# Routed experts on one core: the down products of a step move between the third and fourth quarter of the next step's up products

## The chip, the core and the metric

The kernel runs on one core of a Trainium2 chip, in one launch. The metric is the device time of that core in microseconds (us): the median of several runs, and beside it one profiled execution from which the rows below are read. PE is TensorE, DVE is VectorE, ACT is ScalarE, POOL is GpSimd and SP is SyncE, which only issues DMAs here.

## What is computed

One decoder layer on 1056 tokens (1024 of a prompt, 32 of samples), in fp32. The change touches only the routed experts of the channel-mixing sub-layer:

```python
D_MODEL, N_EXPERTS, TOP_K, EXPERT_FF = 1024, 64, 8, 256

def swiglu(x, w_gate, w_up, w_down):
    return (jax.nn.silu(x @ w_gate) * (x @ w_up)) @ w_down

# in moe(u, ...): eight experts are chosen for each token, gw holds their gates
def expert_block(args):
    xblk, e = args
    return swiglu(xblk, exp_w_gate[e], exp_w_up[e], exp_w_down[e])
yb = lax.map(expert_block, (xb, block_e)).reshape(NB * MOE_BLOCK, D) * buf_w[:, None]
routed = jnp.zeros_like(u_pad).at[buf_t].add(yb)[:T]
```

## The kernel before

The routed tokens are packed into 78 steps of 128 rows (four quarters of 32 rows, "quads"). In a step the first 32 rows belong to one expert, the next 32 to one that may be another, and the last 64 to one that may be a third. Each step n goes through these pieces; the names are those of the functions in `experts`:

- **gather** (POOL): copies the row numbers of the step (L2611) and issues four indirect DMAs (L2616), which fetch the 128 rows into one of NX = 2 buffers. It waits until DVE has transposed the step that used the buffer.
- **turn_x** (DVE, L2835): waits for the gather and transposes the rows into `xT`.
- **up** (PE, L2694 to L2697): gate and up products in one PSUM bank. KT = 8 slices of the 1024 inputs are taken in order, two slices to a "unit", so there are four units (quarters 0 to 3). Four small matmuls of a slice run side by side, one for each quad. The first quad reads the weights where they were loaded (`k.ring`). The other quads read copies: `second_up` (DVE L2873 for units 1 to 3, ACT L2787 for unit 0) and `third_up` (ACT L2788, units 0 to 3). PE waits at the start of each unit for the copies of that unit.
- **silu** (ACT, L2758) and **hidden** (DVE, L2841): silu of the gate half, times the token's gate and the up half.
- **turn_hid** (PE, L2723): transposes the hidden rows; **copy_hid** (ACT, L2799) moves them to SBUF.
- **copies_down** (DVE, L2889, four copies): the down weights of the second and third expert.
- **down** (PE, L2711 to L2714): the down products. PE waits for copy_hid, copies_down and the copy_y of the step before.
- **copy_y** (ACT L2766 one half, DVE L2852 the other): moves the result to `y_out`, which has two buffers; it waits until the add of the step before last has landed.
- **add** (POOL, L2636): an indirect DMA that adds the 128 rows to `y_rows` in HBM. It waits for the landing of the add before it, since two adds may meet in a row.

Every engine's order is written by hand; nothing is scheduled by a tool. On PE the order of one step is turn_hid(n-1), up(n), down(n-1). On DVE it is hidden(n), the three copies for up(n+1), copy_y(n-1), copies_down(n), turn_x(n+2). On ACT it is silu(n), copies for up(n+1) units 0 and 1, copy_y(n-1), copy_hid(n), copies for units 2 and 3. On POOL a gather(n) is followed by add(n-3). Each engine works through its list in order, and a wait holds all that stands behind it.

Which expert a quad uses is known only at run time. So DVE and ACT read slot numbers into registers (`value_load`, L2660, shown as TENSOR_LOAD on the engines' queues DVEq and ACTq). On DVE a step reads five of them, all just ahead of hidden. Steps 2 to 75 run on DVE in a loop of two steps a pass (37 passes), on ACT and PE in similar loops.

Weights come through SP (`reload`): a ring of NW = 4 slots holds gate and up weights, a ring of ND = 5 the down weights. SP waits until the last step of expert e-4 has finished its up products (`up_done`), issues gate and up of expert e (L2115), then reports the expert before, e-1, as ready (`up_ready`, L2554, then `down_ready`) once its loads have landed, waits for `down_done` of expert e-5 and issues the down weights of e. copies_up on ACT and DVE wait for `up_ready` of the newest expert of their step. So an expert becomes ready at the earliest when the last step of the expert three before it has ended its up products.

Of the kernel before, what the change touches and what calls it, by code (L numbers as in the profile page):

```python
# [21 lines left out]
KT = D // P  # L22
# [81 lines left out]
def wait_before_addressed(eng, sem, value, passed):  # L104


    eng.wait_ge(sem, value)
    eng.sem_inc(passed, 1)
# [1840 lines left out]
SLOT = 3 * KT * FF  # L1949
NW = 4  # L1950
# [555 lines left out]
NX = 2  # L2506
# [3 lines left out]
def experts(k):  # L2510
# [35 lines left out]
    with nc.Block() as block:  # L2546
# [57 lines left out]
        def _(g):  # L2604
# [32 lines left out]
                                     in_=y_out[:, u, :], in_offset=None, bounds_check=3 * T - 1, oob_is_err=False, compute_op=ALU.add).then_inc(added, 16)  # L2637

            def run(first, last):
                for n in range(first, first + NX + 1):  # L2640
                    gather(n, n % NX)
                for n in range(first, first + NX - 1):
                    gather(n + NX + 1, (n + 1) % NX)
                    add(n, n % 2)
                loops = (last - first) // NX
                with g.Fori(1, loops - 1) as j:
                    for r in range(NX):
                        gather(j * NX + (first + NX + r), (first + r) % NX)
                        add(j * NX + (first - 1 + r), (1 + r) % 2)
                for n in range(first + loops * NX, last):  # L2650
                    gather(n, n % NX)
                    add(n - NX - 1, (n - 1) % 2)
                for n in range(last - NX - 1, last):
                    add(n, n % 2)
                g.wait_ge(added, 16 * last)
            over_ranges(g, run)
# [18 lines left out]
        def _(pe):  # L2675
# [6 lines left out]
            def up(n, u, off):  # L2682
                pe.wait_ge(x_turned, n + 1)
                gate_up = k.ring[:, bass.ds(off, DOWN)].rearrange("p (g k f) -> p k g f", g=2, f=FF)
                out = ps[:, 2 + u, :].rearrange("p (g f) -> p g f", f=FF)
                for j in range(KT):
                    unit, part = divmod(j, 2)
                    cols = slice(part * FF, (part + 1) * FF)
                    if part == 0:
                        pe.wait_ge(up_by_act, 5 * n + (unit + 2))  # L2690
                        if unit:
                            pe.wait_ge(up_by_dve, 3 * n + unit)
                    edges = dict(start=(j == 0), stop=(j == KT - 1))
                    pe.matmul(out[0:QUAD], xT[:, u, j, 0:QUAD], gate_up[:, j], **edges)  # L2694
                    pe.matmul(out[QUAD:HALF], xT[:, u, j, QUAD:HALF], third_up[unit][:, :, cols], **edges)  # L2695
                    for lo in (HALF, HALF + QUAD):
                        ins = pe.matmul(out[lo:lo + QUAD], xT[:, u, j, lo:lo + QUAD], second_up[unit][:, :, cols], **edges)  # L2697
                    if part and j < KT - 1:
                        ins.then_inc(up_part, 1)
                ins.then_inc(up_done, 1)  # L2700

            def down(n, u, off):
                pe.wait_ge(hid_copied, n + 1)
# [27 lines left out]
            def step(n, u):  # L2731
                off = first_of(n)
                off_before = first_down_of(n - 1)
                turn_hid(n - 1, 1 - u)
                up(n, u, off)
                down(n - 1, 1 - u, off_before)

            def run(first, last):
                up(first, 0, first_of(first))
# [15 lines left out]
        def _(act):  # L2755
# [21 lines left out]
            def registers(n):  # L2777
                return newest_of(act, n), up_offsets_of(act, n)
# [25 lines left out]

            def run(first, last):
                copies_up(first, registers(first), range(4))

                def step(n, u, y=True):
                    regs = registers(n + 1)
                    silu(n, u)  # L2810
                    copies_up(n + 1, regs, (0, 1))
                    if y:
                        copy_y(n - 1, 1 - u)
                    copy_hid(n, u)
                    copies_up(n + 1, regs, (2, 3))
                step(first, 0, False)
                step(first + 1, 1)
                step(first + 2, 0)
                with act.Fori(1, (last - first) // 2 - 1) as j:
                    for r in range(2):  # L2820
                        step(j * 2 + (first + 1 + r), (1 + r) % 2)
                silu(last - 1, 1)
                copy_y(last - 2, 0)
                copy_hid(last - 1, 1)
                copy_y(last - 1, 1)
            over_ranges(act, run)
# [3 lines left out]
        def _(v):  # L2830
# [44 lines left out]
            def copies_up(n, newest, off):  # L2875
                wait_before_addressed(v, up_ready, newest + 1, dve_passed)
                for unit in (1, 2, 3):
                    second_up_unit(n, off, unit)

            def copies_down(n, newest, offs):  # L2880
                wait_before_addressed(v, down_ready, newest + 1, dve_passed)
# [10 lines left out]
            def run(first, last):  # L2892
                turn_x(first, 0, first % NX, first // NX)
                if first == 0:
                    for t in range(SH_DOWN + TAIL_ON_ACT, NT):
                        drain_tail(t)
                copies_up(first, newest_of(v, first), up_offsets_of(v, first)[0])
                turn_x(first + 1, 1, (first + 1) % NX, (first + 1) // NX)

                def step(n, u, x, times, y=True, turn=True):  # L2900
                    newest, offs = newest_of(v, n), down_offsets_of(v, n)
                    newest_up, off_up = newest_of(v, n + 1), column_of(v, n + 1, 0, (NW - 1) * SLOT)
                    hidden(n, u)
                    copies_up(n + 1, newest_up, off_up)
                    if y:
                        copy_y(n - 1, 1 - u)
                    copies_down(n, newest, offs)
                    if turn:
                        turn_x(n + 2, u, x, times)
# [4 lines left out]
                fixed(first, y=False)  # L2914
# [7 lines left out]
                fixed(last - 2, turn=False)  # L2922
                newest, offs = newest_of(v, last - 1), down_offsets_of(v, last - 1)
                hidden(last - 1, 1)
                copy_y(last - 2, 0)
# [187 lines left out]
```

## Time and profile before

| | us |
|---|---|
| median of 3 runs | 2782.24 (2778.79 to 2784.44) |
| the profiled execution's own time | 2782.99 |
| its span, first to last instruction | 2781.2 |
| routed experts: first up product to first up product of the last step | 1811.7 to 2684.5 |
| PE busy over the span | 2620.3 (94%) |

The granted TensorE clock over the span was 0.97 of full speed. The profile is read by stage: what the change is worth lies between 1811 and 2705 us, where PE is the engine with the most work, so the view of what PE waits for there is read first, and then the order of time of one step on each engine.

### The profile page before, as it was taken

To read this page: it belongs to the slowest core of one execution; us is meant where nothing else is said; L and a number is where in the kernel's file an instruction comes from. 1 tells how busy PE (TensorE), PEld (TensorE's weight loads), DVE (VectorE), ACT (ScalarE), POOL (GpSimd) and SP (SyncE) were. 2 spreads that over 40 slices of the span, in tenths; PEclk is the share of its full clock that TensorE was granted. 3 is DMA by queue.
4 is the path that set the end of the run, shared out by engine and by line. 5 is a ranking of instruction groups with operands and counts; after the bars stand their busy time and mean duration, and the time that the engine had idled before them with its cause. 6 is when DMAs were issued, how large, how long until landed. Compare 5 with 4: busy or idle time off the path is not lost. (4 is left out here: it accounts for less than half of the span.)

```text
span 2781.2 us, 48997 instructions
## 1 busy us (share of the span) xinstructions
PE 2620.3 (94%) x16668; PEld 1450.8 (52%) x16669; DVE 1369.1 (49%) x2153; ACT 929.7 (33%) x1404; POOL 730.1 (26%) x860
## 2 busy tenths in 40 slices
PE   7997999998999899999999979899999999999988
PEld 4564888874666656666666646533333333233334
DVE  3333332333757587872211147356666655556644
ACT  3213333333424210001100022155555555555541
POOL 1000211210534100000000001355555555555530
PEclk8998999999989999999999989999999999999998
DMA  6530100011011111211210423299888998999946
GB/s 249 214 121 15 27 16 16 16 54 49 24 31 46 32 35 29 70 35 35 97 34 16 172 90 117 96 315 312 291 280 286 348 338 279 341 309 355 319 109 247
DMA packets 161847, 407.77 MB, mean 147 GB/s; under 512 B 19139, under 2 KB 106255, under 8 KB 133433
## 3 DMA queue, kind: packets, MB, share of 16 engines
q1 hardware_dynamic: 135521, 336.95, 33.0%
q0 software_dynamic: 26208, 69.27, 10.4%
q8 instruction: 71, 1.16, 0.2%
q14 instruction: 47, 0.39, 0.0%
HBM read 343.19 MB, written 75.95 MB: 151 GB/s over the span
## 5 line engine op out<-in xcount | busy, mean ns | idle before, releaser
L2694 PE MATMUL ps<-big 128*32 x1248 | 551.9, 595 | 2.4 <-DVE big L2873 1.6
L2695 PE MATMUL ps<-xT,big 128*32 128x512 f32 x1248 | 551.9, 595 | 0.0
L2616 POOL DMA_INDIRECT big<-u_rows,big x312 | 324.4, 1040 | 139.4 <-issue 71.3
L1760 PE MATMUL ps<-big 128*128 128x352 f32 x1152 | 346.7, 461 | 5.7 <-SPq L1696 5.7
L2788 ACT ACTIVATE xT<-big 128x1024 f32 x312 | 311.0, 1047 | 0.0
L2694 PEld LDWEIGHTS ps<-big 128*32 128x32 f32 x1248 | 136.7, 110 | 332.3 <-issue 332.1
L1760 PEld LDWEIGHTS ps<-big 128*128 128x128 f32 x1152 | 219.7, 191 | 129.1 <-SPq L1696 6.1
L2711 PE MATMUL ps<-big 128*32 x624 | 282.2, 595 | 3.2 <-DVE xT L2889 3.2
L2712 PE MATMUL ps<-xT,big 128*32 128x512 f32 x624 | 282.2, 595 | 0.0
L849 PE MATMUL ps<-big 128*128 128x352 f32 x576 | 205.6, 463 | 2.1 <-DMA big<-in_w_in 2.0
L1304 PE MATMUL ps<-big 128*128 128x352 f32 x576 | 185.2, 469 | 10.2 <-DVE big L1524 7.6
L2636 POOL DMA_INDIRECT y_rows<-big x78 | 140.4, 1800 | 141.3 <-DVE big L2852 99.4
L1774 PE MATMUL ps<-big 128*128 128x352 f32 x576 | 174.4, 459 | 1.6 <-DVE big L1894 1.6
L512 PE MATMUL ps<-big 128*128 128x352 f32 x576 | 173.2, 461 | 0.0
L2711 PEld LDWEIGHTS ps<-big 128*32 128x32 f32 x624 | 68.8, 110 | 190.3 <-issue 190.3
L2841 DVE SCALAR_TENSOR_TENSOR big<-big,ps 128x256 f32<-128x256 f32 x78 | 53.3, 684 | 230.3 <-issue 168.9
L2714 PE MATMUL ps<-pick,big 128*32 128x512 f32 x624 | 161.3, 595 | 0.0
L2714 PE MATMUL ps<-big 128*32 128x512 f32 x624 | 161.3, 595 | 0.0
L2835 DVE STREAM_TRANSPOSE big<-big 128x1024 f32<-128x1024 f32 x78 | 96.8, 1242 | 121.2 <-DMA big<-u_rows,big 121.1
L1864 DVE SCALAR_TENSOR_TENSOR big<-big 128x1024 f32<-128x1024 f32 x120 | 154.0, 1284 | 4.7
L2000 POOL MEMSET big<- 128x1 f32 x1 | 0.1, 98 | 578.3 <-POOLq L1699 578.3
L2758 ACT ACTIVATE big<-ps 128x256 f32<-128x256 f32 x78 | 29.9, 383 | 357.2 <-PE ps L2697 357.2
(621 smaller groups left out, 5038.5 us busy)
## 6 DMA issues: line engine op xcount, KB each, us to landing
big<-in_exp_w_gate SPq DMA_DIRECT2D x64, 1024.0 KB, 6.8
big<-in_exp_w_up SPq DMA_DIRECT2D x64, 1024.0 KB, 9.4
big<-in_exp_w_down SPq DMA_DIRECT2D x64, 1024.0 KB, 10.4
big<-in_ada_w SPq DMA_DIRECT2D x24, 1024.0 KB, 7.8
big<-in_w_in SPq DMA_DIRECT2D x48, 512.0 KB, 4.0
x_keep<-xT SPq DMA_DIRECT2D x2, 4224.0 KB, 16.1
y_rows<-pick SPq DMA_DIRECT2D x16, 512.0 KB, 14.3
big<-y_rows SPq DMA_DIRECT2D x16, 512.0 KB, 12.6
```

The lines of the kernel that those rows point to most:

```text
L512: ins = pe.matmul(ps[:, 3 * u + c, 0:CW], ring[:, s, j, u * P:(u + 1) * P], k.hT[:, j, c * CW:(c + 1) * CW], start=(j == 0), stop=(j == KT ...
L849: ins = pe.matmul(ps[:, F0 + u % 2, 0:CW], ring[:, f % 3, j, :], k.hT[:, j, c * CW:(c + 1) * CW], start=(j == 0), stop=(j == KT - 1))
L1304: ins = pe.matmul(ps[:, bank, 0:CW], ring[:, tile_of[kind, y] % 3, x, :], k.hT[:, x, cs], start=(x == 0), stop=(x == KT - 1))
L1760: ins = pe.matmul(ps[:, c, 0:CW], ring_g[:, q % 2, j, :], k.hT[:, j, c * CW:(c + 1) * CW], start=(j == 0), stop=(j == KT - 1))
L1774: ins = pe.matmul(ps[:, 3 + c, 0:CW], ring_v[:, q % 2, j, :], branch[n][:, j, c * CW:(c + 1) * CW], start=(j == 0), stop=(j == 3))
L2616: g.indirect_dma_start(out=x_rows[:, u, x * 256:(x + 1) * 256], out_offset=None, in_=u_quarters, in_offset=bass.IndirectOffsetOnAxis(idx_i ...
L2694: pe.matmul(out[0:QUAD], xT[:, u, j, 0:QUAD], gate_up[:, j], **edges)
L2695: pe.matmul(out[QUAD:HALF], xT[:, u, j, QUAD:HALF], third_up[unit][:, :, cols], **edges)
L2711: pe.matmul(out[0:QUAD], hidT[:, u, j, 0:QUAD], k.down_ring[:, bass.ds(off + (j * D + half * 512), 512)], **edges)
L2712: pe.matmul(out[QUAD:HALF], hidT[:, u, j, QUAD:HALF], third_down[j][:, cols], **edges)
L2714: ins = pe.matmul(out[lo:lo + QUAD], hidT[:, u, j, lo:lo + QUAD], second_down[j][:, cols], **edges)
L2788: act.activation(third_up[unit], up_columns(third, unit), ACT.Copy).then_inc(up_by_act, 1)
```

## The change

It changes the order of the lists in `experts` and nothing that is computed.

- PE: `up` takes the units that it is to do. A step is now up(n) units 0 and 1, turn_hid(n-1), up(n) unit 2, down(n-1), up(n) unit 3.
- ACT: silu(n), the copy for unit 3 of up(n+1), copy_hid(n), the copies for units 0 to 2 of up(n+2), copy_y(n). It reads registers twice in a step, three values ahead of silu as before and three for step n+2 ahead of copy_hid.
- DVE: hidden(n), the copy for unit 3 of up(n+1), copies_down(n), turn_x(n+2), the copies for units 1 and 2 of up(n+2), copy_y(n). Four registers are read ahead of hidden, two ahead of turn_x.
- POOL: a gather(n) is followed by add(n-4) instead of add(n-3).

```diff
             def run(first, last):
-                for n in range(first, first + NX + 1):
+                for n in range(first, first + NX + 2):
                     gather(n, n % NX)
-                for n in range(first, first + NX - 1):
-                    gather(n + NX + 1, (n + 1) % NX)
-                    add(n, n % 2)
                 loops = (last - first) // NX
                 with g.Fori(1, loops - 1) as j:
                     for r in range(NX):
                         gather(j * NX + (first + NX + r), (first + r) % NX)
-                        add(j * NX + (first - 1 + r), (1 + r) % 2)
+                        add(j * NX + (first - NX + r), r % 2)
...
             def step(n, u):
                 off = first_of(n)
                 off_before = first_down_of(n - 1)
+                up(n, u, off, (0, 1))
                 turn_hid(n - 1, 1 - u)
-                up(n, u, off)
+                up(n, u, off, (2,))
                 down(n - 1, 1 - u, off_before)
+                up(n, u, off, (3,))
...
                 copies_up(first, registers(first), range(4))
-
-                def step(n, u, y=True):
+                copies_up(first + 1, registers(first + 1), (0, 1, 2))
+
+                def step(n, u, next_but_one=True):
                     regs = registers(n + 1)
                     silu(n, u)
-                    copies_up(n + 1, regs, (0, 1))
-                    if y:
-                        copy_y(n - 1, 1 - u)
+                    copies_up(n + 1, regs, (3,))
+                    if next_but_one:
+                        regs = registers(n + 2)
                     copy_hid(n, u)
-                    copies_up(n + 1, regs, (2, 3))
+                    if next_but_one:
+                        copies_up(n + 2, regs, (0, 1, 2))
+                    copy_y(n, u)
...
-                def step(n, u, x, times, y=True, turn=True):
-                    newest, offs = newest_of(v, n), down_offsets_of(v, n)
-                    newest_up, off_up = newest_of(v, n + 1), column_of(v, n + 1, 0, (NW - 1) * SLOT)
+                def step(n, u, x, times, next_but_one=True):
+                    newest, offs, off_up = newest_of(v, n), down_offsets_of(v, n), second_of(n + 1)
                     hidden(n, u)
-                    copies_up(n + 1, newest_up, off_up)
-                    if y:
-                        copy_y(n - 1, 1 - u)
+                    copies_up(n + 1, None, off_up, (3,))
                     copies_down(n, newest, offs)
-                    if turn:
+                    if next_but_one:
+                        newest_up, off_up = newest_of(v, n + 2), second_of(n + 2)
                         turn_x(n + 2, u, x, times)
+                        copies_up(n + 2, newest_up, off_up, (1, 2))
+                    copy_y(n, u)
```

PE inside its loop, before, at the end of a step's up products: the four lines of `carry` are unit 3, and the down products (reading `pick`) follow.

```order
L2697 MATMUL ps<-pair,big 32x512 x2
L2690 REGISTER_ALU
L2692 REGISTER_ALU
L2694 ISA
L2694 MATMUL ps<-big 32x512
L2695 MATMUL ps<-xT,big 32x512
L2697 MATMUL ps<-carry,big 32x512 x2
```

PE after, from the turn (`ident`) to the first down product: unit 2 reads `pair`, and the down products stand right behind it.

```order
L2722 MATMUL ps<-ident,big 32x128 x8
L2688 REGISTER_ALU
L2690 REGISTER_ALU
L2692 ISA
L2692 MATMUL ps<-big 32x512
L2693 MATMUL ps<-xT,big 32x512
L2695 MATMUL ps<-pair,big 32x512 x2
```

So the turn left the head of the step for the middle of the up products, and unit 3 (`carry`) now comes after the down products.

DVE before, second half of a loop pass: copy_y of the step before (`big<-ps`) stands between the up copies and the four down copies.

```order
L2873 COPY carry<-big 128x1024
L2851 ISA
L2852 COPY big<-ps 128x512
L107 REGISTER_ALU
L2889 ISA
L2889 COPY pick<-big 128x1024
```

DVE after, at the end of a loop pass: the two early up copies, then copy_y, then the loop's branch; the four register reads ahead of hidden begin behind it.

```order
L2876 COPY big<-big 128x1024
L2876 ISA
L2876 COPY pair<-big 128x1024
L2854 REGISTER_ALU
L2855 COPY big<-ps 128x512
L2924 REGISTER_ALU
L2924 COMPARE_AND_BRANCH
```

Copy_y moved from the middle of the step to its end, where the reads for the next hidden wait behind it.

ACT after, inside its loop, from copy_hid to copy_y (`big<-ps 128x512`): the first copies for the step after next stand between them, behind the wait for that step's weights, which is held ahead of `pick`.

```order
L2800 ACTIVATE big<-ps 128x256
L107 REGISTER_ALU
L107 ISA
L2788 ISA
L2788 ACTIVATE pick<-big 128x1024
```

Before, the copies at that place were the ones for units 2 and 3 of the next step, whose weights had been waited for earlier:

```order
L2799 ACTIVATE big<-ps 128x256
L2788 ISA
L2788 ACTIVATE xT<-big 128x1024
L2788 ISA
L2788 ACTIVATE xT<-big 128x1024
```

So ACT's wait for weights moved ahead of copy_y(n) and of silu(n+1).

## Rows read from the trace of the kernel before

**Rows 1.** Waits, 1811 to 2700 us: who waited for whom, total, times, longest.

```profile
DVE big L2841 <- issue: 168.9, 55, 4.0
POOL big L2629 <- DMA y_rows<-big: 112.7, 53, 5.1
DVE big L2835 <- DMA big<-u_rows,big: 107.4, 53, 6.0
PE ps L2723 <- DVE big L2841: 33.4, 31, 3.3
ACT pick L2787 <- SPq L2554: 4.4, 4, 1.1
```

**Rows 2.** PE in order of time (start us, us, line): up products and a down product.

```profile
1811.71 0.59 PE L2694 MATMUL ps<-big 128*32 x1
...
2198.36 0.59 PE L2694 MATMUL ps<-big 128*32 x1
...
2209.09 0.59 PE L2694 MATMUL ps<-big 128*32 x1
...
2215.96 0.59 PE L2711 MATMUL ps<-big 128*32 x1
...
2684.47 0.59 PE L2694 MATMUL ps<-big 128*32 x1
```

**Rows 3.** DVE in order of time: transposition and hidden; in brackets idle before, releaser.

```profile
2214.84 1.25 DVE L2835 STREAM_TRANSPOSE big<-big 128x1024 f32<-128x1024 f32 x1 [2.47 <-DMA big<-u_rows,big]
2218.96 0.68 DVE L2841 SCALAR_TENSOR_TENSOR big<-big,ps 128x256 f32<-128x256 f32 x1 [2.87 <-issue]
2219.49 0.68 DVE L2873 COPY big<-big 128x1024 f32 x1
...
2224.81 1.25 DVE L2835 STREAM_TRANSPOSE big<-big 128x1024 f32<-128x1024 f32 x1 [0.44 <-DMA big<-u_rows,big]
2228.46 0.70 DVE L2841 SCALAR_TENSOR_TENSOR big<-big,ps 128x256 f32<-128x256 f32 x1 [2.41 <-ACT big L2758]
```

**Rows 4.** Down on PE, the copy_y it releases, and a down that DVE releases.

```profile
2321.46 0.59 PE L2711 MATMUL ps<-big 128*32 x1
...
2324.46 0.59 PE L2711 MATMUL ps<-big 128*32 x1
...
2325.24 0.69 DVE L2852 COPY big<-ps 128x512 f32<-128x512 f32 x1 [0.43 <-PE ps L2714]
...
2695.63 0.68 DVE L2889 COPY pick<-big 128x1024 f32 x1
...
2697.43 0.92 DVE L2889 COPY xT<-big 128x1024 f32 x1
...
2698.59 0.61 PE L2711 MATMUL ps<-big 128*32 x1 [3.20 <-DVE xT L2889]
```

**Rows 5.** Line L2660, register reads on DVE's queue: count, ns min/median/max.

```profile
L2660 DVEq TENSOR_LOAD <-big x391: 297/306/1580, 1811.9 to 2686.3; - x196
```

**Rows 6.** ACT in order of time at one of its four waits for SP, and silu elsewhere.

```profile
2194.06 0.38 ACT L2758 ACTIVATE big<-ps 128x256 f32<-128x256 f32 x1 [4.46 <-PE ps L2697]
2195.58 1.06 ACT L2787 ACTIVATE pick<-big 128x1024 f32 x1 [1.13 <-SPq L2554]
2196.54 1.04 ACT L2788 ACTIVATE xT<-big 128x1024 f32 x1
...
2216.21 0.38 ACT L2758 ACTIVATE big<-ps 128x256 f32<-128x256 f32 x1 [4.46 <-PE ps L2697]
```

**Rows 7.** PE in order of time: the turn behind one of its longest waits.

```profile
2244.51 0.65 PE L2723 MATMUL ps<-ident,big 128*32 128x128 f32 x16 [3.14 <-DVE big L2841]
```

**Rows 8.** Stretch behind it: us; busy PE, PEld, DVE, ACT, POOL; PE clock; DMA share; GB/s.

```profile
2244.50:2249.00 4.50, 4.49 (x40) 1.59 (x44) 4.50 (x8) 2.28 (x3) 1.49 (x3) 0.64 1.01 405
```

**Rows 9.** POOL in order of time: adds, and an index copy that waits for an add.

```profile
2210.58 1.88 POOL L2636 DMA_INDIRECT y_rows<-big  x1 [1.09 <-DVE big L2852]
...
2220.36 0.45 POOL L2629 COPY big<-big 128x1 int32 x1 [1.85 <-DMA y_rows<-big]
```

More of the change, by code:

```diff
@@ L2648, in run @@
                         gather(j * NX + (first + NX + r), (first + r) % NX)
-                        add(j * NX + (first - 1 + r), (1 + r) % 2)
+                        add(j * NX + (first - NX + r), r % 2)
                 for n in range(first + loops * NX, last):
                     gather(n, n % NX)
-                    add(n - NX - 1, (n - 1) % 2)
-                for n in range(last - NX - 1, last):
+                    add(n - NX - 2, n % 2)
+                for n in range(last - NX - 2, last):
                     add(n, n % 2)
@@ L2680, in first_down_of, with up @@
                 return pe.value_load(k.first_down_tab[0:1, bass.ds(n, 1)], min_val=0, max_val=(ND - 1) * SLOT)
-            def up(n, u, off):
-                pe.wait_ge(x_turned, n + 1)
+            def up(n, u, off, units=range(4)):
+                if 0 in units:
+                    pe.wait_ge(x_turned, n + 1)
                 gate_up = k.ring[:, bass.ds(off, DOWN)].rearrange("p (g k f) -> p k g f", g=2, f=FF)
                 out = ps[:, 2 + u, :].rearrange("p (g f) -> p g f", f=FF)
-                for j in range(KT):
+                for j in [2 * unit + part for unit in units for part in range(2)]:
                     unit, part = divmod(j, 2)
@@ L2699, in up @@
                         ins.then_inc(up_part, 1)
-                ins.then_inc(up_done, 1)
+                if 3 in units:
+                    ins.then_inc(up_done, 1)
             def down(n, u, off):
@@ L2806, in run @@
                 copies_up(first, registers(first), range(4))
[L2808 removed]
+                copies_up(first + 1, registers(first + 1), (0, 1, 2))
+                def step(n, u, next_but_one=True):
                     regs = registers(n + 1)
                     silu(n, u)
[L2811 to L2813 removed]
+                    copies_up(n + 1, regs, (3,))
+                    if next_but_one:
+                        regs = registers(n + 2)
                     copy_hid(n, u)
[L2815 to L2816 removed]
+                    if next_but_one:
+                        copies_up(n + 2, regs, (0, 1, 2))
+                    copy_y(n, u)
+                step(first, 0)
                 step(first + 1, 1)
[L2818 removed]
                 with act.Fori(1, (last - first) // 2 - 1) as j:
                     for r in range(2):
[L2821 removed]
+                        step(j * 2 + (first + r), r)
+                step(last - 2, 0, False)
                 silu(last - 1, 1)
[L2823 removed]
                 copy_hid(last - 1, 1)
@@ L2873, in second_up_unit, with copies_up, second_of @@
                 v.tensor_copy(second_up[unit], up_columns(off, unit)).then_inc(up_by_dve, 1)
-            def copies_up(n, newest, off):
-                wait_before_addressed(v, up_ready, newest + 1, dve_passed)
-                for unit in (1, 2, 3):
+            def copies_up(n, newest, off, units):
+                if 1 in units:
+                    wait_before_addressed(v, up_ready, newest + 1, dve_passed)
+                for unit in units:
                     second_up_unit(n, off, unit)
+            def second_of(n):
+                return column_of(v, n, 0, (NW - 1) * SLOT)
             def copies_down(n, newest, offs):
@@ L2913, in run @@
                 loops = (last - first - 4) // NX
-                fixed(first, y=False)
+                fixed(first)
                 fixed(first + 1)
@@ L2921, in run @@
                     fixed(n)
-                fixed(last - 2, turn=False)
+                fixed(last - 2, next_but_one=False)
                 newest, offs = newest_of(v, last - 1), down_offsets_of(v, last - 1)
                 hidden(last - 1, 1)
-                copy_y(last - 2, 0)
                 copies_down(last - 1, newest, offs)
```

3 lines of the change are left out of this document (2 added, 1 removed).

## The prediction, on record before the changed kernel ran

> **What bounds the kernel now.** I read the waits of the expert stage first [rows 1], then PE in order of time [rows 2], and from PE back to whoever made it wait. In the waits the reader is to see a chain, not one culprit: PE's turn waits for hidden on DVE (33.4 us in 31 waits); DVE's hidden waits not for data but for "issue" (168.9 us, 55 times); ahead of it the transposition waits for a gather (107.4 us, 53 times); and on POOL the next gather stands behind an add that waits for the add before it (112.7 us, 53 times). So a late gather delays the transposition, five register reads follow it, then hidden, and PE's turn comes last.
>
> How much it costs: the first up product of the stage starts at 1811.71, that of the last step at 2684.47 [rows 2], 872.76 us for 77 steps. A step without a wait is the one from 2198.36 to 2209.09: 10.74 us, of which up takes 6.87 (2209.09 to 2215.96), down 3.43 (seven spacings of 0.43 from 2321.46 to 2324.46 [rows 4], and the eighth) and the turn the other 0.43. 77 x 10.74 is 827.0, so **45.8 us** of the stage are PE's waiting. That is all that a new order can win; the work itself is unchanged.
>
> **What the change takes away.** Copy_y, and so the add, no longer waits for a down that stands behind the whole up. The transposition of step n+2 leaves the path to hidden, and an x_rows buffer is given back sooner. A gather stood behind add(n-3), now it stands behind add(n-4). Turn_x(n+2) frees gather(n+4), and nobody needs that before turn_x(n+4), two steps or 21.5 us later, with an add in between whose y is there already; a landing took 9.8 us for an add [rows 9], and turn_x has itself most of a step before PE needs xT. So all 45.8 us go, if nothing new is late. PE's order itself costs nothing: hidden has two up units (3.43 us) to hide under where it had down (3.43 us), and copy_hid has one unit (1.72 us).
>
> **What is late next: a ring through DVE.** Copy_y is now last in DVE's list, waits for down(n), and the four register reads for the next hidden stand behind it; hidden, one up copy and the four down copies follow, and then down(n+1) may start. Round the ring:
> - first to last group of down 3.00 us, and 0.78 from there to copy_y (2324.46 to 2325.24) [rows 4];
> - four reads: a transposition to its hidden is 3.65 us without the loop's branch (2224.81 to 2228.46) and 4.12 with it (2214.84 to 2218.96) [rows 3], for five reads; less one (0.73) it is 2.92 and 3.39;
> - hidden to the next copy 0.53 [rows 3]; that copy 0.60 and three down copies 1.80 (2695.63 to 2697.43), the last 0.69: 3.62;
> - end of the last copy to PE's down 0.24 (2698.35 to 2698.59) [rows 4].
>
> Sum 10.56 us, and 11.03 where the loop's branch lies in it. PE needs 10.74. So one step of each loop pass is 0.29 us too slow: 37 passes, **11 us**. From above: the mean idle before hidden by "issue" is 168.9/55 = 3.07 us [rows 1], against 2.64, the mean of the two rows with and without branch [rows 3], 0.43 more for five reads, 0.34 for four. With that the ring is 10.90 and 11.37, which costs 38 x 0.16 + 37 x 0.63 = 29 us. I take 14, near the lower end: a read's median is 306 ns against a shortest of 297 [rows 5], so most are undisturbed, and the slow ones of before stood beside a running transposition, which these no longer do.
>
> Here the rows have a read at 0.73 us with what belongs to it. The Trainium skill ("DMA: Bandwidth & Descriptors", section "Latency and other measured facts") gives the floor of a tensor_load as about 600 ns; an estimate by that figure has four reads at 2.4 us, the ring at 10.04 and 10.51, under PE's 10.74, and the sum 14 us lower. The rows decide.
>
> **What is late next: weights, four times.** ACT waited for SP's report of weights only four times, 1.1 us at most [rows 1]: in the steps whose newest expert becomes ready only when the up products of the step before have ended. In the order of before this was free: ACT had done silu, and PE had down and turn (3.86 us) ahead of the copies' use. Now up(n+1) follows up(n) directly, and the wait stands ahead of copy_y and of the next silu on ACT, ahead of copy_y and of the next reads on DVE. From the rows, with E 0.25 ahead of silu (2215.96 against 2216.21 [rows 2, 6]): the first copy starts at E+1.77 (2195.58, with silu at 2194.06), the second ends at E+3.77 [rows 6], PE goes on at E+4.0, having stood for 4 us. So down starts 4.0 us late at least. A wait of 3.14 us [rows 7] was followed by a stretch of 4.5 us at a granted clock of 0.64 [rows 8], part of it at the lower level of 1.2 GHz, which cost 0.36 x 4.5 = 1.6 us; that makes 5.6. The hidden behind four held copies points up as well. I take 5.2, four times: **21 us** (16 to 22). A further 2 us (0 to 5) for weights that come late because SP loads two experts in a row; the rows bound this only by the absence of a fifth wait.
>
> Other edits cost nothing. The second set of register reads on ACT lies between its unit 3 copy and copy_hid, where ACT has some 3 us (idle before silu is 4.46 now [rows 6]). The two reads ahead of turn_x run while DVE does the down copies. Start and tail stay: the last down waited 3.20 us for DVE [rows 4]; now copy_y no longer stands ahead of those copies, but down of the step before is no longer there to cover hidden; within 1 us either way.
>
> **Sum.** 2783.0 (the profiled execution's own time; 0.7 above the median of the runs) - 45.8 + 14 + 21 + 2 = 2774.2, so **2774**. It can be told from no change by about 0.2%, that is outside 2776.7 to 2787.8.
>
> **Rivals.**
> 1. The ring does not bind: reads are shorter or run ahead of copy_y. For it: the read itself is only 0.3 us [rows 5]. Against it: hidden at 2218.96 [rows 3] waited for the reads alone, silu having started at 2216.21 [rows 6]. Time 2774 - 14 = 2760. The floor that the Trainium skill gives (named above) would lead here. Chance 0.16.
> 2. The adds keep the pace. Each waits for the landing of the one before, and that took 9.8 us from one add to the index copy of the next (2210.58 to 2220.36 [rows 9]), with the way to the add itself still to come; POOL's waits for it were the second longest of all [rows 1]. At most they set the pace of before, 872.8/77 = 11.33 us a step, which is 2783, with the ring and the weight waits hidden below it. Against it: only 53 of 78 adds waited, and y now comes earlier, so that a slow landing can be made good by quick ones. I price it at 2780, two thirds of the way. Chance 0.16.
> 3. Weights are late in many steps, not four (slower). ACT's wait for `up_ready` comes some 7 us sooner, and copy_y and silu stand behind it. Any expert whose loads land late, hidden today under ACT's idle time, then holds PE for about 5 us. From two such steps beyond the four (2774 + 10 = 2784) the change no longer gains, from three it is measurably slower, and six, the price that I put on it, give 2805. For it: the DMA share in a stretch was 1.01 [rows 8]. Against it: SP is asked three experts ahead. Chance 0.12.
> 4. The ring with slow reads throughout: 2774 + 15 = 2789, slower by a little. Chance 0.10.
> That the change does not do what it says is excluded: the order of the built program has the turn, down and copy_y where it says.
>
> **How the numbers follow.** The forecast, 2766 to 2783 with its own bounds, has 0.46, most of it below 2776.7. Faster by over 0.2%: rival 1, two thirds of the forecast and a little of rival 2, 0.50. Slower by over 0.2%: rivals 3 and 4 and a little of rival 2, 0.23. Within 0.2%: the rest, 0.27. The range leaves out the lower half of rival 1 and nearly all of rival 3: 2757 to 2797.
>
> **What would show it.** Right: DVE's wait for gathers and POOL's share in PE's wait gone; PE's turn without a wait; small PE waits of about 0.3 us before down, every second step, released by the last down copy; four PE waits of about 4 us before the first up product of a step, released by ACT's copy, with SP behind it. The forecast is wrong if the turn still waits, if the reads take under 0.6 us each, if more than six steps wait for SP, or if copy_y waits for an add.

## The result

The changed kernel took **2791.98 us** (median of six runs, 2789.61 to 2796.44) against 2779.74 for the kernel before (six runs beside them): ratio 1.0041, 95% interval 1.003 to 1.0053. It is slower by 0.41%, or 12 us. The forecast was 2774, so it missed by 18 us and in its sign; the range held the time. In a second set on another chip the ratio was 1.0048 (1.0032 to 1.0064).

Of the profiled execution (its own time 2796.44, span 2794.7) first the waits of the expert stage, 1800 to 2710 us (who waits for whom: total us, times, longest). Lines have moved: up is L2692 to L2695, down L2710 to L2713, the turn L2722, transposition L2838, hidden L2844, copy_y L2855 on DVE and L2767 on ACT, copies_down L2896.

```profile
POOL big L2629 <- DMA y_rows<-big: 110.6, 57, 5.0
...
ACT pick L2788 <- SPq L2554: 43.3, 6, 9.1
...
PE ps L2710 <- DVE xT L2896: 18.9, 35, 1.9
PE ps L2692 <- ACT xT L2789: 17.4, 5, 3.8
DVE big L2838 <- DMA big<-u_rows,big: 13.8, 1, 13.8
...
PE ps L2722 <- DVE big L2844: 1.8, 2, 1.2
```

Against [rows 1]: the transposition waited 53 times for a gather, now once, for the first. PE's turn waits (33.4 us in 31) are down to 1.8 us in two. In their place PE waits ahead of down for DVE's last down copy (18.9 us, 35 times) and ahead of up for ACT's copies (17.4 us, five times), with ACT behind SP. The adds wait for one another as before.

Then one turn of the ring, DVE, ACT and PE in order of time (start us, length us; in brackets idle before and releaser), against [rows 3, 4]:

```profile
2017.71 0.69 DVE L2855 COPY big<-ps 128x512 f32<-128x512 f32 x1 [1.72 <-PE ps L2713]
...
2019.89 0.39 ACT L2759 ACTIVATE big<-ps 128x256 f32<-128x256 f32 x1 [1.59 <-PE ps L2695]
...
2021.23 0.69 DVE L2844 SCALAR_TENSOR_TENSOR big<-big,ps 128x256 f32<-128x256 f32 x1 [2.82 <-ACT big L2759]
...
2024.19 0.96 DVE L2896 COPY xT<-big 128x1024 f32 x1
...
2024.24 0.59 PE L2692 MATMUL ps<-big 128*32 x1
...
2025.39 0.61 PE L2710 MATMUL ps<-big 128*32 x1 [0.53 <-DVE xT L2896]
```

Copy_y to hidden takes 3.52 us; the row names ACT as releaser, but silu had ended at 2020.28, and the four reads in between are what ends last. The last down copy ends at 2025.15, down starts 0.24 later and PE has stood for 0.53. From the group before, at 2024.24, to down at 2025.39 are 1.15 us where 0.43 is normal: the wait cost 0.72, which is 0.19 more than its recorded length.

Last the step with number 48, one of the five that waited for weights (SP, ACT and PE in order of time, and the stretch behind: us; busy PE, PEld, DVE, ACT, POOL; PE clock; DMA share; GB/s), against [rows 6, 8]:

```profile
2352.73 0.33 SPq L2115 DMA_DIRECT2D big<-in_exp_w_gate  x1
...
2353.95 1.06 ACT L2788 ACTIVATE pick<-big 128x1024 f32 x1 [8.36 <-SPq L2554]
2354.91 2.93 ACT L2789 ACTIVATE xT<-big 128x1024 f32 x3
2357.75 0.58 ACT L2767 ACTIVATE big<-ps 128x512 f32<-128x512 f32 x1
...
2356.09 0.65 PE L2692 MATMUL ps<-big 128*32 x1 [3.63 <-ACT xT L2789]
...
2356.00:2360.50 4.50, 4.41 (x28) 1.31 (x32) 1.75 (x4) 3.55 (x5) 1.18 (x1) 0.62 1.02 424
```

SP issues the next expert's loads first, and only then reports the expert that ACT waits for. ACT's copies follow, PE stands 3.63 us and then runs 4.5 us at a granted clock of 0.62, that is partly at the lower level of 1.2 GHz, which costs (1 - 0.62) x 4.5 = 1.7 us more. Copy_y on ACT comes behind the held copies.

### The profile page after: what moved, and what is told of

Same layout as the page of the kernel before. It is cut to its first block and busy times, and to the rows that moved or that the text cites. A ratio compares the mean times of both kernels' runs of the same rounds, so it can differ in the third digit from the quotient of the medians.

```text
span 2794.7 us, 50064 instructions
## 1 busy us (share of the span) xinstructions
PE 2632.9 (94%) x16668; PEld 1458.4 (52%) x16669; DVE 1359.6 (49%) x2153; ACT 934.5 (33%) x1404; POOL 739.7 (26%) x860
## 5 line engine op out<-in xcount | busy, mean ns | idle before, releaser
L2692 PE MATMUL ps<-big 128*32 x1248 | 571.2, 599 | 22.0 <-ACT xT L2789 17.4
L2693 PE MATMUL ps<-xT,big 128*32 128x512 f32 x1248 | 571.3, 599 | 0.0
L2692 PEld LDWEIGHTS ps<-big 128*32 128x32 f32 x1248 | 136.9, 111 | 353.5 <-issue 352.2
L2710 PE MATMUL ps<-big 128*32 x624 | 284.4, 599 | 19.3 <-DVE xT L2896 18.9
L2711 PE MATMUL ps<-xT,big 128*32 128x512 f32 x624 | 284.7, 599 | 0.0
L2710 PEld LDWEIGHTS ps<-big 128*32 128x32 f32 x624 | 64.4, 110 | 219.5 <-issue 218.5
L2713 PE MATMUL ps<-pick,big 128*32 128x512 f32 x624 | 163.5, 602 | 0.0
L2713 PE MATMUL ps<-big 128*32 128x512 f32 x624 | 161.7, 596 | 0.0
L2844 DVE SCALAR_TENSOR_TENSOR big<-big,ps 128x256 f32<-128x256 f32 x78 | 53.4, 685 | 208.3 <-ACT big L2759 181.5
L2695 PE MATMUL ps<-pick,big 128*32 128x512 f32 x624 | 153.3, 613 | 0.0
L2695 PE MATMUL ps<-big 128*32 128x512 f32 x624 | 149.4, 598 | 0.0
## 6 DMA issues: line engine op xcount, KB each, us to landing
big<-y_rows SPq DMA_DIRECT2D x16, 512.0 KB, 12.7
```

Of the source, the lines that this page charges most:

```text
L2710: pe.matmul(out[0:QUAD], hidT[:, u, j, 0:QUAD], k.down_ring[:, bass.ds(off + (j * D + half * 512), 512)], **edges)
L2711: pe.matmul(out[QUAD:HALF], hidT[:, u, j, QUAD:HALF], third_down[j][:, cols], **edges)
L2713: ins = pe.matmul(out[lo:lo + QUAD], hidT[:, u, j, lo:lo + QUAD], second_down[j][:, cols], **edges)
```

## The experiments

Ratios are against the kernel before, measured on the same chip in the same set; in brackets the 95% interval.

### The ring

**Reads ahead of copy_y.** DVE's copy_y(n) moves behind the four reads of the next step:

```diff
 newest, offs, off_up = newest_of(v, n), down_offsets_of(v, n), second_of(n + 1)
+if y:
+    copy_y(n - 1, 1 - u)
 hidden(n, u)
...
-copy_y(n, u)
```

> The changed kernel with one difference: on DVE copy_y(n) is put behind the four register reads of step n+1 instead of ahead of them. Theory (the ring binds): PE stood 19.3 us ahead of down in 38 steps of the changed kernel, and the granted clock fell a little after each; without the reads (2.92 to 3.39 us) the ring takes some 7.5 us against PE's 10.74, so these waits go, all but the last down's (1.87). From 2792 that is 2772 (2766 to 2776); the waits for weights (five of about 3.5 us ahead of up) stay. Rival (the waits ahead of down come from DMA traffic or from the adds, not from the reads): within 4 us of 2792, and the waits stay where they are.

Measured 2782.0, ratio 1.0012 [0.9995, 1.0029]: 10 us off instead of 20. Its waits:

```profile
DVE big L2855 <- DMA y_rows<-big: 48.2, 14, 4.4
...
PE ps L2692 <- ACT xT L2789: 16.1, 5, 3.7
PE ps L2710 <- DVE xT L2896: 13.0, 19, 1.9
```

The small waits of every second step are gone (19 waits instead of 35, most of them in steps 52 to 65), but copy_y now waits for adds, which it hardly did in the changed kernel, and holds hidden and the down copies behind it. The ring cost something, and behind it stands another limit.

**One read more.** A fifth read ahead of hidden:

```diff
 newest, offs, off_up = newest_of(v, n), down_offsets_of(v, n), second_of(n + 1)
+newest_of(v, n)
 hidden(n, u)
```

> The changed kernel with a fifth register read (the first one a second time, its value unused) behind the four that stand between copy_y and hidden on DVE. Theory (a ring through these reads sets the pace): an undisturbed ring of the changed kernel is 10.56 us, and 11.15 with the loop's branch; 0.73 more makes 11.29 and 11.88 against PE's 10.74, that is 1.69 instead of 0.41 us per pass of two steps, 1.28 x 38 = 49 us more: 2841 (2825 to 2850), with PE waiting ahead of nearly every down. Rival (PE's waits ahead of down come from DMA traffic, and reads are cheap): 2792 to 2800.

Measured 2827.1 (two runs), ratio 1.017 [1.0137, 1.0202]. Copy_y and hidden of one step, and PE's wait:

```profile
2026.69 0.69 DVE L2855 COPY big<-ps 128x512 f32<-128x512 f32 x1 [1.72 <-PE ps L2713]
2030.82 0.68 DVE L2844 SCALAR_TENSOR_TENSOR big<-big,ps 128x256 f32<-128x256 f32 x1 [3.44 <-issue]
...
PE ps L2710 <- DVE xT L2896: 47.4, 70, 1.1
```

A step with the loop's branch now has 4.13 us between the two (2026.69 to 2030.82) where it had 3.51: the read costs 0.61, not the 0.73 that I had used. By that the loss is 2 x 0.61 for a pass, less the 0.18 of slack that the undisturbed ring without branch had: 1.04 x 38 = 40; it was 35. So reads do sit in the ring that paces PE, and with four of them it binds: rival 1 did not come. The Trainium skill ("DMA: Bandwidth & Descriptors", section "Latency and other measured facts") gives about 600 ns as the floor of a tensor_load. The trace does not agree: a read by itself is recorded with 297 ns at least and 305 in the median, and the 0.61 us of one read more hold the register operations that go with it.

### The reports of weights

**Report first.** SP reports gate and up of expert e-1 before it waits for the place of e; nothing else moves:

```diff
 e, x = i * GROUP + (NW + r), NW + r
+report_up((x - 1) % NW, loads_of(i, x - 1, NW))
 wait_before_addressed(sp, up_done, end_of(i * GROUP + r), sp_passed)
 load_part(k, sp, e, x % NW, 0)
 load_part(k, sp, e, x % NW, 1)
-ready((x - 1) % NW, loads_of(i, x - 1, NW), x % ND, loads_of(i, x, ND) - (x % ND == 0))
+report_down(x % ND, loads_of(i, x, ND) - (x % ND == 0))
```

> The changed kernel with one difference: SP reports the up weights of expert e-1 before it waits for a free place for expert e, where it did so after having issued those loads. Theory (the report stood behind a wait for the last use of an older expert): the four PE waits of 3.6 to 3.8 us ahead of up in steps 35, 48, 67 and 68 go, with 7 us of lowered clock behind three of them, so 2792 becomes 2771 (2768 to 2778); the wait in step 39, where two experts are loaded in a row, stays or grows by up to 4 us, since the second load is now issued later. Rival (the weights themselves land late in these steps): the four waits stay, 2792, or more by what the later issue costs, up to 2800.

Measured 2778.8, ratio 0.9997 [0.9987, 1.0007]: 13 us off instead of 21. PE's waits for ACT ahead of up fall from 17.4 us to these:

```profile
PE ps L2699 <- ACT xT L2796: 7.0, 4, 3.1
```

Steps 48 and 68 no longer wait; 35 waits 1.0, 67 waits 2.5, and 39 waits 3.1 instead of 2.6. In 67 the weights themselves are late, which the four equal waits had hidden: SP does nothing there but wait for them to land, from 2551.84 to its report at 2558.42.

**Both.** 

> Both differences together. Theory: two costs that lie in different steps add up, 20 and 21 us off 2792, so 2751 (2743 to 2760), which is faster than the kernel before (2780) by 1%. Rival (a third limit stands close behind, for instance the adds, which need a step of 11.2 us in the mean): 2770 or more, with DVE's or ACT's copy_y waiting for an add.

Measured 2770.6, ratio 0.9965 [0.9953, 0.9978]; the two gains nearly add up (10 and 13, together 21), but not to 2751. The time is at its rival's bound, and DVE's copy_y does wait for adds (20.6 us, 9 times). The worst place (ACT, PE, two load issues of SP, and a window of the same columns as above):

```profile
2534.39 0.33 SPq L2115 DMA_DIRECT2D big<-in_exp_w_gate  x1
...
2546.10 0.33 SPq L2115 DMA_DIRECT2D big<-in_exp_w_gate  x1
...
2557.06 1.06 ACT L2795 ACTIVATE pick<-big 128x1024 f32 x1 [11.16 <-SPq L2554]
...
2559.20 1.06 PE L2699 MATMUL ps<-big 128*32 x1 [6.88 <-ACT xT L2796]
...
2500.00:2600.00 100.00, 92.75 (x960) 31.22 (x956) 60.51 (x88) 51.84 (x68) 56.17 (x61) 0.97 1.00 348
```

Here every step has a new expert. The DMA queues are busy all the time, experts are issued 11.3 to 11.7 us apart, and PE needs 10.74 for a step. The weights fall behind until PE stands for 6.88 us. The edit has a part in this spacing: with the report first, SP issues an expert's gate and up only when those of the expert before have landed. How large that part is, no run here shows.

### Traffic

**Small adds.** The changed kernel, where an add carries 32 rows of 128 and leaves the other 96 out of the result:

```diff
-out_offset=bass.IndirectOffsetOnAxis(idx_out[:, u:u + 1], 0), in_=y_out[:, u, :],
+out_offset=bass.IndirectOffsetOnAxis(idx_out[0:32, u:u + 1], 0), in_=y_out[0:32, u, :],
```

> The changed kernel with adds of 32 of the 128 rows of a step (the other rows of y are not added to the result): 128 KB instead of 512 KB for each add, everything else as it is. Theory (reads and reports hold PE, not traffic): the waits ahead of down (19 us) and the four of 3.6 us ahead of up stay, and only disturbed register reads get quicker: 2780 (2774 to 2790). Rival (full DMA queues are behind both): waits ahead of down under 10 us in all, and 2768 or less.

Measured 2776.8, ratio 0.9992 [0.9982, 1.0003]. Waits, the register reads on DVE's queue (ns min/median/max), and a window; under them the same line and window of the changed kernel:

```profile
PE ps L2710 <- DVE xT L2896: 14.9, 36, 1.9
PE ps L2692 <- ACT xT L2789: 14.6, 4, 3.7
L2657 DVEq TENSOR_LOAD <-big x467: 297/303/549, 1812.4 to 2690.9; - x156
2500.00:2600.00 100.00, 91.78 (x896) 28.91 (x892) 54.18 (x80) 48.68 (x64) 52.71 (x56) 0.93 0.80 294
```

```profile
L2657 DVEq TENSOR_LOAD <-big x467: 297/305/1574, 1810.1 to 2705.0; - x156
2500.00:2600.00 100.00, 88.29 (x892) 28.20 (x888) 53.76 (x79) 47.81 (x63) 55.18 (x57) 0.98 0.98 339
```

With a DMA share of 0.80 instead of 0.98 no read takes longer than 549 ns, only the four steps 35, 48, 67 and 68 wait for weights, and the time is the forecast's within 3 us. The waits of the ring and of the reports are there with less traffic too. That the time is so near the forecast is in part luck: by the table below these waits still cost more than the forecast had (45 us against 37), and the gain was larger than it had too.

**Both, with small adds.** 

> The kernel with both differences (reads ahead of copy_y, weights reported before the wait for a free place), 2771, with adds of 32 of the 128 rows, as above. Theory (with the ring and the reports out of the way, traffic is what is left: weights of single-step experts landing late in steps 35, 39 and 67, and copies of y that wait for an add): the waits ahead of up fall from 16.6 us to under 8, copy_y waits for no add, and the time is 2747 (2738 to 2755). Rival (something else, such as DVE's or ACT's own work): 2765 to 2771.

Measured 2743.6, ratio 0.9869 [0.9843, 0.9894]. PE's waits ahead of up are 4.5 us:

```profile
DVE big L2862 <- DMA y_rows<-big: 61.7, 28, 2.8
PE ps L2717 <- DVE xT L2903: 6.2, 6, 1.9
PE ps L2699 <- ACT xT L2796: 4.5, 5, 1.8
```

The time is as expected; that copy_y would wait for no add is not what the first row says, but PE no longer pays for it. The edit takes away bytes and shortens the chain of adds at once, so this run does not tell the two apart.

**The changed kernel again.** 

> The changed kernel itself a second time, since its profile is of the slowest of its six executions (2796 of 2790 to 2796). Theory (register reads are held up by traffic, by chance of the moment): the 13.2 us by which reads between copy_y and hidden were longer than their median change from one execution to another, and the four waits of 3.6 to 3.8 us ahead of up and the waits of 0.2 to 0.5 us ahead of every second down do not; so a profile of a 2790 us execution shows reads longer by 8 us or less in all and waits ahead of down of some 16 us instead of 19.3. Rival (the slow reads belong to the program, to certain steps of it): the same steps are slow again, 11 to 15 us in all.

Measured 2792.3, ratio 1.0048 [1.0032, 1.0064]; the profiled execution is the median one.

```profile
PE ps L2710 <- DVE xT L2896: 18.2, 37, 1.9
L2657 DVEq TENSOR_LOAD <-big x467: 297/304/1434, 1809.6 to 2702.1; - x156
```

Neither expectation is quite met. The reads between copy_y and hidden were 10.5 us longer than at their median, between 8 and 11, and mostly in the same steps as the first time (3, 9, 22, 42, 52, 54, 60). So it is not chance alone: in these steps a read is held up each time, and with small adds it is not.

Read by read, the traces tell more. Of the 55 reads that begin 0.5 to 3 us behind the record of an add on POOL, 26 take over 400 ns in this run; of the other 412 only 6 do. Full queues alone do not do it: in "POOL's part and those reads" below, the DMA share from 1900 to 2600 us is 0.94 against 0.91 here, and 7 of 391 reads take over 400 ns, all of them among the 40 that begin in that stretch. With adds of 128 KB 2 of 174 do ("Both, with small adds"; in "Small adds" itself only 2 reads begin there). So what holds a read up goes with a 512 KB add that has just been issued.

### Where the expected gain went

**POOL's part alone.** The kernel before with the changed order on POOL, the other engines as they were:

```diff
 gather(j * NX + (first + NX + r), (first + r) % NX)
-add(j * NX + (first - 1 + r), (1 + r) % 2)
+add(j * NX + (first - NX + r), r % 2)
```

> The kernel before with POOL's part of the change alone: gather n stands behind add n-5 rather than n-4; PE, ACT and DVE keep the order of before. Theory (the late gather was the first cause of PE's turn waits): DVE's transposition no longer waits for gathers; from one down to hidden of the next step but one are then 0.24 + 2.5 (copies) + 2.3 (transposition) + 4.1 (reads) + 0.5, under PE's 10.74 a step, so the 34.6 us of turn waits and most of the 13 us of lowered clock go: 2780 becomes 2742 (2735 to 2755). Rival (the order on PE and DVE was needed for it: the transposition and five reads ahead of hidden are too long even with the gather there, or the adds keep the pace): 2770 to 2782, and PE still waits ahead of the turn.

Measured 2769.1, ratio 0.9961 [0.9947, 0.9975]: faster by 11 us, a third of what I expected.

```profile
DVE big L2838 <- issue: 117.0, 41, 3.8
DVE big L2832 <- DMA big<-u_rows,big: 78.6, 46, 14.2
ACT big L2763 <- DMA y_rows<-big: 74.8, 42, 3.4
PE ps L2720 <- DVE big L2838: 12.7, 18, 3.7
PE ps L2691 <- ACT xT L2785: 10.5, 16, 1.2
```

The turn waits fall from 33.4 to 12.7 us, but a new one of 10.5 has come in the middle of up: ACT's third-expert copies stand behind copy_y, and copy_y waits for an add.

**The order without POOL's part.** 

> The changed kernel with POOL's order of before (gather n behind add n-4): the order part of the change alone. POOL's part alone took 11 us off the kernel before. Theory A (in the new order copy_y comes earlier and the transposition has most of a step to spare, so a gather that comes a step later is hidden): 2792, within 5. Theory B (the two parts add up): 2792 + 11 = 2803, and DVE's transposition waits for gathers again.

Measured 2795.4, ratio 1.0051 [1.0033, 1.0069], theory A in the time. The transposition does wait for gathers again (117.7 us, 49 times), yet PE's waits are of the same two kinds as in the changed kernel (17.7 us ahead of down, 14.8 ahead of up). So the new order on PE, DVE and ACT is what loses, 16 us against the kernel before, and POOL's part gains little in it.

**Reads behind hidden, in the kernel before.** Hidden itself needs none of the five reads:

```diff
-newest, offs = newest_of(v, n), down_offsets_of(v, n)
-newest_up, off_up = newest_of(v, n + 1), column_of(v, n + 1, 0, (NW - 1) * SLOT)
 hidden(n, u)
+newest_up, off_up = newest_of(v, n + 1), column_of(v, n + 1, 0, (NW - 1) * SLOT)
 copies_up(n + 1, newest_up, off_up)
+newest, offs = newest_of(v, n), down_offsets_of(v, n)
```

> The kernel before with one difference: on DVE the five register reads stand behind hidden (two ahead of the up copies, three behind them) instead of ahead of it. Theory (what the change could win lay in two links of one chain, the late gather and the reads behind the transposition; POOL's part alone removed the first and won 11 us): hidden no longer waits for reads, so most of the turn waits go (34.6 us in 38 steps, down to 12 or so), and copies of y that wait for adds come up instead: 2780 becomes 2765 (2758 to 2772). Rival (the gather alone decides, the reads only follow it): 2775 to 2782.

Measured 2788.4, ratio 1.0023 [1.0006, 1.004]: slower. Hidden's wait for reads is gone, but the transposition's for gathers grew from 107.4 to 196.4 us:

```profile
DVE big L2835 <- DMA big<-u_rows,big: 196.4, 62, 13.9
PE ps L2723 <- DVE big L2841: 40.4, 30, 5.0
```

All five reads now stand between hidden and DVE's copy_y. From the last down product of a step to that copy it takes 3.37 us in the median instead of 2.35, so the add, and with it the gather behind it on POOL, can come later. That this is the whole loss is not shown; a part of DVE's idle time has only moved from hidden to the transposition.

**POOL's part and those reads.** 

> The kernel before with POOL's part of the change and the five reads behind hidden. Theory: of the PE waits that POOL's part alone left, 13.3 us ahead of the turn (with about 4 us of slow restarts) go but for the last steps' 5; 9.7 us in the middle of up, where ACT's copies stand behind a copy of y that waits for an add, stay: 2769 becomes 2757 (2750 to 2763). Rival (adds and full queues keep the pace at 11.1 us a step whatever the order): 2766 to 2772, the waits only move to the middle of up.

Measured 2765.8, ratio 0.995 [0.9933, 0.9966], the lowest median of the complete kernels here, though its interval overlaps those of "Both" and of "POOL's part alone". Waits, and POOL in order of time:

```profile
ACT big L2763 <- DMA y_rows<-big: 86.2, 46, 3.7
PE ps L2691 <- ACT xT L2785: 20.5, 21, 1.9
PE ps L2720 <- DVE big L2838: 1.2, 1, 1.2
...
2239.25 1.98 POOL L2636 DMA_INDIRECT y_rows<-big  x1 [1.08 <-DVE big L2849]
2249.80 0.18 POOL L2629 COPY big<-big 128x1 int32 x1 [2.19 <-DMA y_rows<-big]
2251.05 2.00 POOL L2636 DMA_INDIRECT y_rows<-big  x1 [1.07 <-DVE big L2849]
```

As its rival had it, in time and place: the turn no longer waits, and the wait in the middle of up has doubled. From one add to the index copy that waits for its landing are 10.55 us, to the next add 11.80. Over all 78 adds the spacing is (2687.9 - 1836.4)/77 = 11.06, from the first and last of this line:

```profile
L2636 POOL DMA_INDIRECT y_rows<-big x78: 1577/1849/2143, 1836.4 to 2687.9; - x78
```

**And ACT's copy_y behind all up copies.**

```diff
-copies_up(n + 1, regs, (0, 1))
+copies_up(n + 1, regs, range(4))
 if y:
     copy_y(n - 1, 1 - u)
 copy_hid(n, u)
-copies_up(n + 1, regs, (2, 3))
```

> As the one before, and on ACT copy_y(n-1) stands behind all copies of up weights for step n+1, ahead of copy_hid. Theory: the waits in the middle of up (9.7 us and their restarts) go too: 2744 (2738 to 2752), the time that the kernel with both differences had only with small adds. Rival (adds keep the pace): the copies of y wait as long, now ahead of silu or of down, and the time is 2757 or more.

Measured 2780.5, ratio 0.999 [0.9965, 1.0016], with executions from 2755 to 2793. The wait has gone from up to down:

```profile
DVE big L2848 <- DMA y_rows<-big: 96.6, 42, 4.8
PE ps L2708 <- DVE xT L2885: 25.6, 20, 3.0
```

DVE's copy_y waits for the same adds, and the down copies stand behind it. Moving the place where an add is met gained nothing here; against the run before it cost 15 us.

## Why the prediction was wrong

**Right: the chain of before and its end.** The gather waits, POOL's share in them and the turn waits went, as the first two steps said (2.0 us of turn waits are left). "The order without POOL's part" adds that the new order alone would have freed PE from the turn waits.

**Right in kind, too small in size: both new waits.** This is the step that failed: in the sum the ring stood with 14 us and measured 24, the four waits for weights with 21 and measured 25, and 2 us stood for everything else that is new, which measured 10. Against them stood a gain of 45.8 us that was 49. Gain and loss are nearly equal, so an error of this size in the loss turned the sign. What was to be seen was seen: waits of 0.2 to 0.6 us ahead of every second down, and waits of 3.6 to 3.8 us in the four steps whose weights had been waited for before. Of the signs listed as refuting it there are only traces: two short turn waits, and copy_y waiting for an add not at all in the first profile and twice in the second (3.5 us on DVE).

From the first up product to the first one of the last step the stage took 882.2 us in the median execution (1809.38 to 2691.61), 18.2 more than the 827.0 + 37 = 864 of the forecast, which is the whole miss. The 827.0 is too high: the stretch holds 77 ups but only 76 downs (and after the change 76 turns), so PE's own work in it is 823.1 us, 823.5 before, and PE's waiting before was 49.2 us, not 45.8. The terms were 22.1 us too small together; the 3.9 by which the 827.0 is too high hid a part of that. From PE in order of time, group of matmuls by group:

| us | forecast | small adds | changed (2792.3) |
|---|---|---|---|
| waits ahead of down, without the last | 14 | 13.0 in 35 | 16.6 in 39 |
| restart behind them | in the 14 | 6.7 | 7.4 |
| four waits for weights | 21 | 14.6 | 14.6 |
| restart and lowered clock behind them | in the 21 | 7.7 | 10.7 |
| other waits of up and turn, with restart | 2 | 1.1 | 6.5 |
| the rest, mostly pieces under 0.2 us | 0 | 2.0 | 3.3 |
| sum; measured: stage less 823.1 | 37 | 45.1 | 59.1 |

- *The ring, 14 against 24.* Of the 14, 11 were 0.29 us for each of 37 passes, from one down to the next. With small adds, where the reads are undisturbed, that step takes 11.30 us in the median, not 11.03. Two legs were too short. The loop's branch is worth 0.60 us (3.51 against 2.91 from copy_y to hidden), not 0.49. And the four down copies stood with 2.49 us, because the last one got the 0.69 of another copy; [rows 4] has 0.92 for it and 2.72 for the four (2695.63 to 2698.35), and in the waiting steps they take 2.6 in the mean. Each of the two is worth some 4 us. The recorded waits are shorter than what PE loses by about 0.19 each, because a matmul of 0.59 us otherwise overlaps the next, which starts 0.43 behind it; the sum, taken from start to start, holds this already, the expected sign of 0.3 us does not. And reads were 10.5 us longer, of which 4.4 reach PE (24.0 against 19.6 with small adds): I had put the slow reads of [rows 5] down to the running transposition and therefore dropped them. That was not the cause, or not the only one. The transposition no longer stands beside them and they are slow all the same, behind an add. The upper bound, 29, held.
- *Weights, 23 against some 32.* The four steps were right, and their waits (3.63 to 3.78) a little shorter than the 4.0 of the forecast. What follows them was priced from one row of 1.6 us; behind step 35 the granted clock was 0.50 for 4.5 us and 0.87 for as long again, which is 2.8. Step 39 (two loads in a row) was a fifth in the first profile, 2.64 us, and 0.70 in the second; waits of 0.5 to 1.0 us ahead of up came in five more places, which the 2 us for the rest did not cover.

**Wrong too, though not what failed here: how much there was to win.** "All that a new order can win" took PE's 10.74 us a step as the floor. The adds are slower than that. In "POOL's part and those reads" they follow one another 11.1 us apart from the first to the last, while PE takes 10.76 us a step from step 2 to step 34 and so runs ahead of them; all its waits in the middle of up come from step 34 on, and from there to step 76 a step takes 11.34. An add starts there in the median 10.9 us behind the end of its copy_y, against 0.9 in the kernel before, so it is not y that is late. The stage took 853.7 us (1811.17 to 2664.87), 858.8 with both differences, against 872.8 before: some 19 us were won. That is no limit either: one execution of "And ACT's copy_y behind all up copies" took 2755.3, 9 us less than the fastest of "POOL's part and those reads". Rival 2 named this mechanism, an add that waits for the landing of the one before, and copies of y wait for adds wherever the rest is cleared away: DVE's in "Reads ahead of copy_y", ACT's in "POOL's part alone" and "POOL's part and those reads", DVE's again in the last run. I gave it 0.16, for the reason that only 53 of 78 adds waited. That is no argument: where the adds are the limit it is 58. In the changed kernel itself the adds hardly hold PE (copy_y waits for down, not for an add); ring and weights come first.

What stays open: whether the adds take 11.1 us because each waits for the landing of the one before, or because of the bytes on the queues (share 0.9 to 1.0 in the stage). Small adds relieve both. And why a register read is slow just behind an add of 512 KB is not shown, only that it is.

## What to carry over

Before a gain is written down as all of an engine's idle time, look for the second clock of the loop: here a chain of DMAs, each waiting for the landing of the one before, at about 11.1 us against PE's 10.74. Where a forecast is the difference of two sums of like size, a few tenths of a microsecond in a leg that comes round 38 times decide its sign. An order that takes the cover off a late report or a row of register reads pays for it in small waits, and each of them costs more than its recorded length; in the changed kernel doing the reads ahead of the wait took 10 us off, sending the reports ahead of it 13. Move one engine's part alone first: POOL's part was the one that gained, 11 us.

## What was not expected of the hardware

- Register reads on DVE's queue have a median of 305 ns and reach 1574 ns in the changed kernel, in mostly the same steps in two executions; with a quarter of the adds' bytes the longest is 549. Taken one by one, 31 of 467 exceeded 400 ns, against 3. The slow ones begin 0.5 to 3 us behind an add: 26 of 55 there and 6 of 412 elsewhere in the second execution, 23 of 60 and 8 of 407 in the first.
- The clock behind nearly equal waits differs: after 3.63 us of standing (step 48) 0.62 over 4.5 us, after 3.78 us (step 35) 0.50 over 4.5 us:

```profile
2200.70:2205.20 4.50, 4.48 (x24) 1.20 (x28) 1.84 (x4) 3.47 (x5) 0.66 (x2) 0.50 1.00 403
2205.20:2209.70 4.50, 4.50 (x54) 1.50 (x48) 3.90 (x6) 2.05 (x3) 1.88 (x2) 0.87 0.99 373
```

The first of these stretches of the changed kernel is at the lower level, 1.2 GHz, throughout.
